# Changing how the second layer's mixer builds its gated linear attention and its latent attention

## The reference, cut to what matters

```python
u = x @ od_w_in
gq, gk, gv, g_low, gr, c_q, c_kv, k_r = split_cols(u, ODD_SPLITS)
# gated linear attention, for s <= t, b the running sum of the log gates:
log_a = log_sigmoid(g_low @ w_gate + b_gate) / 16
o[t] = sum over s <= t of (q[t] * exp(b[t] - b[s]) * k[s]) summed over 64 channels, times v[s]
o = rms_norm(o, g_norm) * silu(gr)
# latent attention: q = rms_norm(c_q) @ w_uq, k and v = rms_norm(c_kv) @ w_ukv, rotary parts,
# causal softmax over 256 keys, times v
y = concatenate([o, latent], -1) @ od_w_out
x = layer_norm(ALPHA * x + y);  x = layer_norm(ALPHA * x + swiglu(x))
```

## Time and profile before

| | |
|---|---|
| median of 3 runs | 980.71 us |
| the profiled execution | 981.14 us, span 979.3 us |
| TensorE busy | 912.6 us (93%) |
| VectorE, ScalarE, GpSimd busy | 700.8, 503.2, 109.8 us |
| odd mixer, first matmul to the first of the next stage | 627.64 to 766.23: 138.6 us |
| TensorE idle in it, waits added up | 22.7 us |

### The profile page before, as it was taken

How to read it: one execution, slowest core, us unless ns; L and a number is a source line. 1 busy time by engine, 2 the same in 40 slices (tenths; PEclk the granted TensorE clock), 3 DMA queues, 4 the chain that set the end, 5 groups by cost and what they waited for, 6 DMA issues and landing times.

```text
span 979.3 us, 19204 instructions
## 1 busy us (share of the span) xinstructions
PE 912.6 (93%) x7270; PEld 889.4 (91%) x7270; DVE 700.8 (72%) x1174; ACT 503.2 (51%) x744; POOL 109.8 (11%) x101
## 2 busy tenths in 40 slices
PE   6989799999998999999999999995879799999996
PEld 5969799999998999899999999995769799999995
DVE  5866897777778746879766666976886576666667
ACT  6345443433443546775655555656536455555553
POOL 1000100000000022008000000303401460000001
PEclk9999899999998999999999999996999989999997
DMA  8853265556552654434655555434113155555531
GB/s 290 282 197 108 71 194 183 178 191 193 185 184 84 215 175 148 131 110 160 220 179 172 190 193 178 133 125 156 56 44 114 60 172 185 181 181 182 175 127 43
DMA packets 43992, 155.24 MB, mean 159 GB/s; under 512 B 5071, under 2 KB 5673, under 8 KB 43945
## 3 DMA queue, kind: packets, MB, share of 16 engines
q1 hardware_dynamic: 42192, 151.12, 47.0%
q10 hardware_dynamic: 1305, 1.87, 0.6%
q0 software_dynamic: 448, 1.59, 0.5%
HBM read 153.50 MB, written 1.06 MB: 158 GB/s over the span
## 4 chain that ended last, share of the span: by engine, by line
PE 80%; DVE 8%; ACT 4%; issue 3%; POOL 2%; DMA 1%; ACTq 0%; SPq 0%; POOLq 0%; DVEq 0%
PE ps L414 23%; PE ps L416 23%; PE ps L415 23%; DVE w_lo L1278 1%; PE ps L438 1%; PE ps L431 1%; POOL x L329 1%; PE ps L432 1%; PE ps L791 1%; PE ps L510 1%; ACT w_hi L926 1%; PE ps L491 1%; DMA raw<-in_stream 1%; PE ps L473 1%; PE ps L475 1%
## 5 line engine op out<-in xcount | busy, mean ns | idle before, releaser
L414 PE MATMUL ps<-op_hi,w_hi 128*128 128x258 f32 (+1 forms) x1324 | 375.0, 283 | 0.0
L416 PE MATMUL ps<-op_hi,w_lo 128*128 128x258 f32 (+1 forms) x1324 | 373.6, 282 | 0.0
L415 PE MATMUL ps<-op_lo,w_hi 128*128 128x258 f32 (+1 forms) x1324 | 373.0, 282 | 0.0
L1278 DVE TENSOR_TENSOR w_lo<-raw,w_hi 128x1024 fp32r<-128x1024 f32 x224 | 275.4, 1249 | 38.9 <-ACT w_hi L926 38.4
L926 ACT ACTIVATE w_hi<-raw 128x1024 fp32r<-128x1024 f32 x224 | 230.9, 1050 | 72.0 <-PE ps L416 54.4
L414 PEld LDWEIGHTS ps<-op_hi,w_hi 128*128 128x128 f32 x1324 | 249.8, 189 | 1.2 <-DVE w_lo L1278 0.8
L415 PEld LDWEIGHTS ps<-op_lo,w_hi 128*128 128x128 f32 x1324 | 250.8, 189 | 0.1
L416 PEld LDWEIGHTS ps<-op_hi,w_lo 128*128 128x128 f32 x1324 | 249.9, 189 | 0.0
L414 PE MATMUL ps<-mix_hi,w_hi 128*128 128x256 f32 x768 | 224.0, 292 | 14.3 <-issue 5.5
L415 PE MATMUL ps<-mix_lo,w_hi 128*128 128x256 f32 x768 | 220.5, 287 | 0.0
L416 PE MATMUL ps<-mix_hi,w_lo 128*128 128x256 f32 x768 | 220.3, 287 | 0.0
(11 more groups left out here) (267 smaller groups left out, 941.0 us busy)
## 6 DMA issues: line engine op xcount, KB each, us to landing
raw<-in_stream SPq DMA_DIRECT2D x284, 512.0 KB, 3.8
x<-in_x SPq DMA_DIRECT2D x4, 256.0 KB, 6.1
bias<-bias_rows POOLq DMA_DIRECT2D x1, 1024.0 KB, 8.5
result<-x SPq DMA_DIRECT2D x4, 256.0 KB, 2.0
bias<-bias_rows POOLq DMA_DIRECT2D x1, 512.0 KB, 10.6
proj<-in_gmask ACTq DMA_DIRECT2D x1, 512.0 KB, 5.7
masks<-in_masks ACTq DMA_DIRECT2D x1, 384.0 KB, 5.1
wpool<-in_wpool ACTq DMA_DIRECT2D x1, 256.0 KB, 4.6
```

The source lines that it names most:

```text
L414: pe.matmul(o, wh, xh, start=start, stop=False, **kw)
L415: pe.matmul(o, wh, xl, start=False, stop=False, **kw)
L416: return pe.matmul(o, wl, xh, start=False, stop=stop, **kw)
L1278: m = dve.tensor_tensor(w_lo[:, s, :], raw[:, s, :], fp(w_hi[:, s, :]), ALU.subtract)
```

## The change

In the odd mixer:

- The running sum and GpSimd's subtractions go. The log gates are made token-major, with the bias as a 33rd row of `w_gate`, and TensorE multiplies them with constant 0/1 matrices (`spans`) that give each level's exponent; ScalarE exponentiates straight from PSUM.
- VectorE makes keys and queries of a level in one instruction (`faded_pair`), and the level matmuls take one head per half of the array (64 rows), with only the right halves as columns: eight small products a level in place of four of 256 columns. The masked copy covers the right halves only.
- The chunks come as misc, gq, gk, c_q, c_kv, two of gr, the four of gv, the q unit, one of gr, the k/v unit, the last of gr; levels and spans lie between the chunks. All but the last two gr chunks use the unnormalised operand.
- The residual x is made by GpSimd (`normed_x`), and centred in the middle of the mixer.
- The latent heads go as two pairs (`pair_shift` and so on), with gla's units of `od_w_out` first as filler; the single-head `attention` is gone.
- `scan0` (128 KB) leaves the late constants, `spans` (576 KB) enters, `w_gate` grows from 16 to 33 rows.

```diff
         late_consts = [("wpool", wpool[:]), ("masks", masks[:]), ("p", pt[:]), ("rope", rope[:]), ("gmask", gmask_f),
-                       ("scan0", scan0[:]), ("w_gate", w_gate[:])]
+                       ("spans", spans[:]), ("w_gate", w_gate[:])]
...
+            pool.memset(faded[0], 0.0).then_inc(S["faded_cleared"], 1)
...
+            normed_x("ln_ffn_g", "ln_ffn_b", 0, 3)
+            inverse_root(6)
             pool.wait_ge(S["vop_lo"], 4)
+            centre_x(3)
...
+            first, second = slice(0, 64), slice(64, 128)
+            def span(i):
+                if i == 1:
+                    pe.wait_ge(S["gate_summed"], 1)
+                elif i > 2:
+                    pe.wait_ge(S["fade"], i - 2)
                 for a in range(2):
                     for t in range(2):
+                        m = pe.matmul(bank(6 + i % 2, a * SEQ + t * P, P), log_gate[:, t * SEQ + a * P:t * SEQ + a * P + P],
+                                      spans[:, i - 1 if i < 8 else 7 + t, :], start=True, stop=True)
+                m.then_inc(S["span_done"], 1)
+            def diagonal():
+                pe.wait_ge(S["evac"], EV_ODD + 5)
+                for b in range(4):
+                    for h, r in enumerate((first, second)):
+                        m = pe.matmul(bank(4 + h, b * P, P), key_query[r, b * P:b * P + P],
+                                      key_query[r, 512 + b * P:512 + b * P + P], start=True, stop=True)
+                m.then_inc(S["level_done"], 1)
...
+            def level(i):
+                pe.wait_ge(S["faded"], i)
+                pe.wait_ge(S["level_kept"], i)
+                kq, m = faded[i % 2], LEVELS[i]
+                for b in range(4):
+                    for h, r in enumerate((first, second)):
+                        q = right(kq[r, 512 + b * P:512 + b * P + P], m)[:, 0]
+                        mm = pe.matmul(right(bank(4 + h, b * P, P), m)[:, 0], kq[r, b * P:b * P + P], q, start=True, stop=True)
...
+            for c in range(10):
+                if c >= 3:
+                    pe.wait_ge(S["evac"], EV_ODD + c - 2)
                 if c == 0:
                     pe.wait_ge(S["z_ready"], 8)
+                    first_chunks(bank(0, 0, SEQ + 2), bank(1, 0, SEQ + 2), 5, *raw_operand)
                     square_mean(6)
                 if c == 2:
                     spread([(0, 6, SEQ), (1, 6, SEQ + P)])
+                if c == 3:
+                    for t in range(2):
+                        m = pe.matmul(bank(7, t * SEQ, SEQ), proj[0:33, 2, t * P:t * P + P], w_gate[:], start=True, stop=True)
                     m.then_inc(S["gate_z"], 1)
+                if c >= 2:
+                    out_chunk(bank(c % 3, 0, SEQ + 2), *raw_operand)
+                if c == 5:
+                    diagonal()
+                    span(1)
+                    span(2)
+                if c > 5:
+                    level(c - 5)
+                    span(c - 3)
             pe.wait_ge(S["mla_sq"], 1)
+            token_means(1, [(0, 1, [sq[:, 4, :], sq[:, 5, :]]), (2, 2, [sq[:, 6, :]])])
+            pe.wait_ge(S["evac"], EV_ODD + 9)
+            pe.wait_ge(S["vop_lo"], 4)
+            token_unit(512, mix_hi, mix_lo, 0, 2, False, banks=(2, 3))
             level(5)
+            span(7)
+            spread([(j, 1, j * P) for j in range(4)])
+            token_unit(512, mix_hi, mix_lo, 2, 2, False, banks=(2, 3))
+            level(6)
+            span(8)
+            token_unit(512, mix_hi, mix_lo, 4, 2, False, banks=(2, 3))
+            level(7)
+            pe.wait_ge(S["evac"], EV_ODD + 10)
+            mean_of_x(chunk(0, 0))
+            token_unit(512, mix_hi, mix_lo, 6, 2, True, banks=(2, 3))
+            across()
...
+            pe.wait_ge(S["level_kept"], 9)
+            pe.wait_ge(S["v_copied"], 1)
...
+            pe.wait_ge(S["fade"], 8)
+            out_chunk(chunk(7, 0), mix_hi, mix_lo)
+            pe.wait_ge(S["gla_sq"], 2)
+            token_means(4, [(2 * h, 2, [sq[:, h, :]]) for h in range(GLA_H)])
...
+            gla_filler(0, 18, 0)
+            pe.wait_ge(S["gr_done"], 4)
+            mla_scores(0)
+            pe.wait_ge(S["gla_normed"], 2)
+            gla_filler(0, 18, 1)
+            mla_scores(1)
+            gla_filler(1, 18)
+            pair_turn(8, 18)
+            gla_filler(2, 20)
+            mla_values(0)
+            gla_filler(3, 20, 0)
+            pair_turn(9, 20)
+            gla_filler(3, 20, 1)
+            pe.wait_ge(S["mix_ready"], 22)
+            mla_values(1)
+            mix_filler(4, 22)
+            mix_filler(5, 22)
+            mix_filler(6, 24)
+            mix_filler(7, 24)
...
+            def fade(i):
+                act.wait_ge(S["span_done"], i)
                 if i > 2:
+                    act.wait_ge(S["faded"], i - 2)
+                act.activation(gee[:, i % 2, :], bank(6 + i % 2), ACT.Exp, scale=1.0 / GLA_TAU).then_inc(S["fade"], 1)
...
+            act.activation(proj[:, 11, :], chunk(5, 0), ACT.Silu).then_inc(S["gr_done"], 1)
+            pair_exp(8, False)
+            step()
+            step()
+            pair_exp(9, False)
+            pair_copy(8)
+            step()
+            step()
+            pair_copy(9)
+            for _ in range(4):
+                step()
...
+            def faded_pair(i):
+                m = (LEVELS + (128,))[i]
+                dve.wait_ge(S["fade"], i)
+                if i == 2:
+                    dve.wait_ge(S["faded_cleared"], 1)
                 if i > 2:
                     dve.wait_ge(S["level_done"], i - 1)
+                dve.tensor_tensor(by_half(faded[i % 2], m, 512), by_half(gee[:, i % 2, :], m, 0), by_half(key_query, m, 512),
+                                  ALU.mult).then_inc(S["faded"], 1)
...
+            gla_gate(0)
+            causal = over(masks[:, 0, :], 2)
+            pair_shift(8, causal, False)
+            gla_gate(1)
+            step()
+            step()
+            pair_scale(8, False)
+            pair_shift(9, causal, False)
+            step()
+            pair_scale(9, False)
+            step()
+            def mla_mix(p):
+                dve.wait_ge(S["pair_summed"], 9 + p)
+                put_mix(4 + 2 * p, 2, ps[:, 4:6, 0:SEQ])
+            mla_mix(0)
+            step()
+            step()
+            mla_mix(1)
```

More of the change, by code:

```diff
@@ L1787, in _ @@
             turned_k = y[lo_q, 0:3, :]
-            own.done(dve.memset(att, 0.0))
-            places = (2, 0, 1, 3, 8, 9, 10, 11, 4, 5, 6, 7)
-            for c in range(12):
+            places = (2, 6, 7, 4, 5, 0, 1, 3, 8, 9)
+            for c in range(10):
                 step()
@@ L1816, in _ @@
                                           ).then_inc(S["vop_lo"], 1)
[L1817 to L1822 removed]
+                if c == 8:
                     own.done(dve.tensor_tensor(turned_k[:, 0, :], proj[lo_q, 2, :], cos, ALU.mult))
```

634 lines of the change are left out of this document (216 added, 418 removed).

## The result

The changed kernel takes 969.39 us (median of four, 967.86 to 971.81), the kernel before 980.75 beside it: a ratio of 0.9887 (95% interval 0.9865 to 0.9910), 11.3 us less. The profiled execution is the slowest of the four, 971.81 us with a span of 969.0.

A forecast was written before the change was run, and what follows sets the result against it. TensorE, busy in nine tenths of nearly every slice, was taken to set the end. Work +3.1, waits -5.9, clock -0.3, end -1.9 and -1.5, constants +2.0 gave -4.5 us: 976.2, range 970.5 to 985.0.

The forecast's parts named there:

- TensorE's work: Odd mixer: levels and cross product go, eight spans and half-array levels come; +3.1 us net.
- The two long waits of the pair stretch: TensorE waits 3.0 us before the first unit of `od_w_out` and 5.3 before the first turn.
- the waits: TensorE's waits in the odd mixer, by following the four engines' lists at full clock: 18.3 us, 5.9 less than before.
- the 1.2 before the fourth chunk and 1.8 before the first level: Odd mixer: TensorE waits charged for VectorE slowed beside GpSimd's residual and sum of x; bounds 0 and double.
- the half-array levels: Odd mixer's seven levels: 1.0 us each if halves overlap, 1.7 if not; 1.3 added for all seven.
- the end: Next stage's start: wait 1.5 us in place of 3.4 (-1.9), operand start 5.85 in place of 7.3 (-1.5).
- the reason for the first two waits: Waits of 4.4 and 5.6 us go because no running sum or subtraction stands between chunk and level.
- the 5.7 at level 6: TensorE's 5.7 us wait before level 6 goes with the doubled copies.
- The clock: Odd mixer: 4 us lost at half clock in place of 6.5, counted as -0.3 us.
- The rule of three quarters: Odd mixer: three quarters of the time lost to slow clock is won back in waits.
- The rival that had the clock at half through the pair stretch: From before gla's spread to the second turn, half clock costs +9.5 us: 985.7; chance 0.17.
- The rival of shorter waits: Pair stretch: waits shorter than walked, ScalarE early with splits, and less slow clock; -4.5 more: 971.7; chance 0.16.

The follow-up runs named there:

- the three profiles: The changed kernel's first profile (executions' median 969.39 us) and two more runs of the same file without edit, 968.95 and 968.08 us.
- the second profile: The changed kernel run anew without edit, as control: 968.95 us, ratio 0.9872 to the kernel before.
- the experiment: Changed kernel with diagonal, levels and cross product issuing one array half's products, then the other's, instead of alternately: 974.10 us, ratio 0.9920.
- The experiment on the kernel before: Kernel before with four silus, the softplus and the first level's exponential moved behind splits in ScalarE's list: 972.47 us, ratio 0.9912.
- the kernel kept busy: Kernel before with unread products on TensorE in two long waits, 34 before the ninth chunk, 44 before the first token unit: 980.68 us, ratio 0.9998.
- the mean of x copied early: Kernel before with ScalarE's copy of the mean of x behind the third of the last seven splits instead of the seventh: 975.08 us, ratio 0.9944.
- the scale first: Changed kernel with the first pair's pair_scale and second's pair_shift ahead of two low parts, sixth head chunk ahead of two others: 962.53 us, ratio 0.9812.
- the gate first: Changed kernel with one VectorE low part moved from ahead of gla's norm and gate to behind the first gate: 961.04 us, ratio 0.9801.
- the reordered kernel before: Kernel before with silus, softplus and first exponential behind splits, and the copy of the mean of x ahead of the last four splits: 968.14 us, ratio 0.9856.
- its repairs: Changed kernel with 0/1 matrices behind the awaited constants, gla's gate ahead of a low part, first pair's scale ahead of two: 952.16 us, ratio 0.9719.

## Why the forecast was right in direction and too small

**Right.** TensorE's work: forecast +3.1, and the mixer's difference less waits and half clock leaves +2.1 to +2.6 (135.2 less 19.3 of wait and 6.6 lost at half clock is 109.3; 125.9 less 10.6 and 3.4 is 111.9). This is in part luck: the spans cost 1.09 each in place of 0.95, 1.1 more for all eight, and the 1.3 added for the levels wasn't needed. The constants: +2.0, measured +1.3 over all traces. The two long waits of the pair stretch: 3.0 and 5.3 walked, 3.39 and 4.48 measured, and both for the reason given, a low part behind a centred split ahead of the instruction that TensorE needs. The waits of 1.1 before the third chunk and 0.3 at the mix came as walked. The start of the next stage from its first matmul to the statistic takes 5.8 us, as forecast. There is no wait over 2 us between 660 and 700.

**Mis-sized, the waits.** This is the step of the forecast that failed most. It had the waits fall by 5.9 us, from 24.2 walked to 18.3 walked; they fell by 8.7, 9.2 and 8.6, from 19.3 to 10.6, 10.1 and 10.7. Of the 5.8 to 8.9 us by which the three profiles beat the forecast this is 2.7 to 3.3, the gap at the next stage 1.5 and the work 0.5 to 1.0, in each of them; the rest is half clock, the start and the end, and differs from profile to profile. (The four short waits of before, too, are 3.55 us in sum and not the 3.3 that the prediction has.) The terms of the walk that weren't there are
- the 1.2 before the fourth chunk and 1.8 before the first level, charged for GpSimd beside VectorE: 3.0, measured 0. The contention is real and larger than charged (5.0 us of VectorE's time), but a delay of VectorE was put on TensorE's account without asking for the lead of two chunks that TensorE leaves it. The run with the residual off GpSimd was no faster. Nor is GpSimd idle beside all of the new `faded_pair`, as the prediction says: the first one (658.97) takes 1.40 us beside the sum of x, a later one 0.68;
- the 0.4 after the sixth chunk, 1.8 for gla's root (0.75), 0.3 and 1.0 for bank and copy (none), 2.0 for the second turn (0.65, none in the second profile), 5.3 (4.48). In part this is the walk at full clock: two half-clock stretches lie over the scores and behind the turn (721.5 to 724.9 and 735.2 to 738.6), TensorE's own work stretches there and waits can shrink by as much. The walk of before was 4.9 us over its trace with 6.6 lost at half clock; that of after is 7.7 and 8.2 over with 3.4 and 6.0 lost. If the same three quarters are put down to the clock, some 4 to 5 us are the walk's own error, by estimate.

**Mis-sized, the half-array levels.** 1.3 us were added for halves that don't overlap; the level is 1.04 and the experiment shows the overlap. The middle between two bounds was taken where the nearest row, the paired score, had the answer. The Trainium skill, "TensorEngine Tiling (Array Packing)", section "Performance Considerations", warns against tiling where a dimension is already small, since a matmul has a floor; by that the forecast had priced its upper end of 1.7 us a level. Here the records of one half after the other cost 0.096 us each (1.54 / 16) and those of alternate halves 0.065: alternating saves a third even so, and the measurement decides.

**Mis-sized, the end.** The forecast was 1.9 for the gap and 1.5 behind it; measured were 3.4, and 2.9, 2.2 and 1.1 behind it. The reference row was wrong: the odd mixer's own start, where VectorE is late with the last chunk of the stage before. Behind `od_w_out` it is free at 755.9, forms the first pair of y at 757.03, under the last unit, and nothing is waited for. The chance to see it was in the profile of before: the copy of the mean at 758.2 had its input since 744.4.

**Wrong in the main, the reason for the first two waits.** The 4.4 and 5.6 went, as forecast; but the forecast had them go since "no running sum, no subtraction stands between chunk and level". The experiment on the kernel before keeps all of that and loses one wait wholly and the other by 2.2. So 6.6 of the 10.0 us were made by the order of ScalarE's list. What makes the 3.4 that are left isn't settled; the running sum is one candidate. In the changed kernel ScalarE starts the softplus (645.97) after 5.0 us without work, with the splits done ahead, and the silus wait until 703. That the 5.7 at level 6 went with the doubled copies was argued and not tested; the contention with the sum of x is the larger part by the estimate above.

**The clock, taken at too little.** The forecast took 4 us as lost at half clock (3.4, 6.0 and 4.5 by the profiles), but counted only 0.3 of the fall from 6.5, since three quarters would come back as waits; a quarter of 2.5 is 0.6, so the term is off by its own numbers too. The rule of three quarters doesn't hold by itself. Before a chain that other engines set, all is won back (the kernel kept busy, 0.9998). Where TensorE is the bound, nothing is: the mean of x copied early and the scale first show it, the gate first suggests it. The rival that had the clock at half through the pair stretch was to decide from about 10 us of it on. From gla's spread to the last wait the granted clock was 0.90, 0.85 and 0.86 in the three profiles, with 6.8, 10.2 and 10.2 us at half, so its condition was just met twice. Its price wasn't: these two executions took 970.0 and 967.7 us, not 985.7. The rival of shorter waits, 971.7, was the nearest.

Of the gain itself: with two moves in ScalarE's list the kernel before takes what the changed kernel takes. The new arithmetic by itself adds 2.1 to 2.6 us to TensorE and 1.3 to 2.0 of constants. What the change as a whole has that the reordered kernel before lacks is a mixer without the level-6 wait of 5.7 us. The changed kernel with its repairs goes to 952.2. Whether the old arithmetic with like repairs of its latent heads would get there wasn't tried.

## What to carry to other kernels

Ask of each long wait which instruction stands ahead of the releaser in its own engine's list, and whether that one is needed now: work done ahead (a weight split) belongs behind what the busiest engine is waiting for, and ahead of what itself has to wait. Charge a delay of a helper engine only beyond the lead that it has. In these runs half clock behind a wait cost in full where TensorE was the bound, and nothing where its next wait was set by other engines.

## What the runs showed of the hardware that was not expected

- The start of one file differs from execution to execution: in the second profile of the changed kernel the slow clock of the start ends at 14.8 us, in the first at 25.2 (with 3.4 us of full clock from 18.4 on), 3.7 us of time; in the kernel before it ends at 13.3. The Trainium skill, "TensorE: Matmul & The Clock Gate", Part 1, says that the number of slow matmuls at the start varies from run to run; the traces agree.
- VectorE beside GpSimd: an fp32 `tensor_scalar` from SBUF to SBUF took 0.36 or 1.02 us, a `tensor_tensor` with two inputs in SBUF 1.21 or 2.31. The 2.31 starts at 647.41, beside the last of GpSimd's four products, which end at 648.63; from there 1.09 are left, about its time alone. The product that reads PSUM stayed at 0.41 to 0.42 throughout. The Trainium skill, "SBUF — State Buffer", section "SBUF: two separate sides", has the loser wait for the other's whole instruction; this one case agrees.
- An fp32 product of 64 rows and 64 columns (two records) costs 0.130 us where the halves alternate (1.04 / 8) and 0.19 where one half follows the other (1.54 / 8).
